# A fused transformer step on one core: the order and the loads of 128 value tiles, with 88 early tiles instead of 64 and whole rows for their second reading

## The reference

```python
def peer_ffn(h, w_query, sub_keys, expert_u, expert_v):
    def block(hb):                                   # 128 tokens
        ...                                          # 8 heads x 16 best of 16,384 experts
        idx = jnp.take_along_axis(cand_i, best_j, axis=-1)
        gate = jax.nn.softmax(best_s, axis=-1)
        u = expert_u[idx]
        act = jax.nn.gelu(jnp.einsum('thkd,td->thk', u, hb))
        coef = (gate * act)
        return jnp.einsum('thk,thkd->td', coef, expert_v[idx])
...
x = x + gt2 * ffn
y = rmsnorm(x, g_final)
```

## Time and profile before

| | us |
|---|---|
| median of 3 runs (lowest, highest) | 3785.51 (3781.29, 3787.98) |
| the profiled execution: its own time | 3779.13 |
| its span | 3777.4 |

### The profile page before, as it was taken

How to read it: one execution, slowest core, us unless ns; L and a number is a source line. 1 busy time by engine, 2 the same in 40 slices (tenths; PEclk the granted TensorE clock), 3 DMA queues, 4 the chain that set the end, 5 groups by cost and what they waited for, 6 DMA issues and landing times.

```text
span 3777.4 us, 28728 instructions
## 1 busy us (share of the span) xinstructions
PE 3104.6 (82%) x9975; PEld 1850.8 (49%) x9975; DVE 2353.0 (62%) x3580; ACT 572.1 (15%) x1365; POOL 980.1 (26%) x779
## 2 busy tenths in 40 slices
PE   4899997979996668796885885359996589999996
PEld 1333443733343434333674553347773257777774
DVE  3110114889986854548777777877777838656653
ACT  0000111121111445402242000420000000000000
POOL 3000001234333421233313323333223314222220
PEclk8999998979998679897996997579998899999998
DMA  9999655889989799988989999889999989999993
GB/s 310 398 361 367 233 200 202 338 319 403 409 330 361 262 401 415 397 296 336 367 292 358 416 416 386 283 341 417 417 417 416 416 333 417 416 417 417 417 411 132
DMA packets 326129, 1344.80 MB, mean 356 GB/s; under 512 B 27625, under 2 KB 76777, under 8 KB 217593
## 3 DMA queue, kind: packets, MB, share of 16 engines
q0 software_dynamic: 106912, 749.72, 49.8%
q1 hardware_dynamic: 166090, 549.84, 37.9%
q10 hardware_dynamic: 52984, 43.42, 3.5%
HBM read 1303.07 MB, written 38.96 MB: 355 GB/s over the span
## 4 chain that ended last, share of the span: by engine, by line
PE 57%; DMA 20%; DVE 15%; issue 4%; ACT 3%; POOL 0%; SPq 0%; ACTq 0%; DVEq 0%; POOLq 0%
PE ps L1023 27%; PE ps L619 7%; DVE arena L2183 7%; DMA arena<-in_expert_u_dram,arena 6%; DMA arena<-in_expert_v_dram 5%; PE ps L778 4%; PE ps L828 4%; DMA arena<-in_cache_k_dram 3%; PE ps L710 3%; PE ps L577 2%; DMA arena<-in_w_ada_dram 2%; DMA arena<-in_w_in_dram 2%; PE ps L607 2%; PE ps L1015 2%; DMA arena<-in_w_out_dram 1%
## 5 line engine op out<-in xcount | busy, mean ns | idle before, releaser
L1023 PE MATMUL ps<-arena 128*128 128x512 f32 x3072 | 1384.4, 611 | 175.2 <-DMA arena<-in_expert_v_dram 116.1
L2183 DVE CUSTOM_DVE_ANT_0 arena<-arena 128x2048 f32<-128x2048 f32 x544 | 1241.7, 2290 | 315.3 <-DMA arena<-in_expert_u_dram,arena 309.5
L1023 PEld LDWEIGHTS ps<-arena 128*128 128x128 f32 x3072 | 943.6, 309 | 615.0 <-issue 270.9
L2448 POOL DMA_INDIRECT arena<-in_expert_u_dram,arena x544 | 760.6, 1398 | 1760.9 <-DVE arena L2183 1567.0
L2096 DVE SCALAR_TENSOR_TENSOR arena<-arena 128x2048 f32<-128x2048 f32 x158 | 371.6, 2352 | 205.3 <-issue 165.8
L828 PE MATMUL ps<-arena 128*128 128x512 f32 x896 | 409.4, 611 | 0.4 <-DVE arena L2027 0.2
L619 PE MATMUL ps<-arena 128*128 128x512 f32 x640 | 288.4, 604 | 9.5 <-DMA arena<-in_w_in_dram 9.5
L828 PEld LDWEIGHTS ps<-arena 128*128 128x128 f32 x896 | 169.7, 195 | 246.6 <-issue 240.1
L2448 POOL DMA_INDIRECT arena<-in_expert_v_dram,arena x160 | 176.7, 1105 | 410.5 <-DVE arena L2096 368.3
L577 PE MATMUL ps<-arena 128*128 128x128 f32 (+3 forms) x954 | 158.4, 319 | 151.7 <-DMA arena<-in_cache_k_dram 50.3
L577 PEld LDWEIGHTS ps<-arena 128*128 128x128 f32 (+3 forms) x954 | 128.0, 169 | 220.2 <-issue 67.7
(11 more groups left out here) (246 smaller groups left out, 1761.1 us busy)
## 6 DMA issues: line engine op xcount, KB each, us to landing
arena<-in_expert_v_dram SPq DMA_DIRECT2D x320, 512.0 KB
arena<-in_w_ada_dram SPq DMA_DIRECT2D x96, 1024.0 KB, 10.5
arena<-in_w_in_dram SPq DMA_DIRECT2D x80, 1024.0 KB, 8.2
arena<-in_w_query_dram SPq DMA_DIRECT2D x36, 1024.0 KB
arena<-dense_coefs SPq DMA_DIRECT2D x48, 768.0 KB
arena<-in_w_out_dram SPq DMA_DIRECT2D x32, 1024.0 KB, 5.1
dense_coefs<-arena ACTq DMA_DIRECT2D x12, 2048.0 KB, 20.4
arena<-in_cache_k_dram SPq DMA_DIRECT2D x24, 1024.0 KB
```

The costliest lines, as they stand in the source:

```text
L1023: ins = MM(ps[:, BANK[half, b] + c, :], weights, dense_v[m % V_DENSE][:, c * NC:(c + 1) * NC], start=(m == FIRST_TILE[half, b]), stop=(m = ...
L2183: V.tensor_tensor_reduce(out=u_slot[s % RING], in0=u_slot[s % RING], in1=h2[b], scale=1.0, scalar=0.0, op0=ALU.mult, op1=ALU.add, accum_ou ...
L2448: nc.gpsimd.indirect_dma_start(out=slot, out_offset=None, in_=table, in_offset=bass.IndirectOffsetOnAxis(ap=idx, axis=0),).then_inc(loaded ...
```

## The change

There are now 88 early tiles. The list is: 88 lower tiles for blocks 0 and 1; the other 40 lower tiles for all three; then for each of the first 88 groups a pair, its lower columns for block 2 and its upper columns for all three, loaded as one transfer of whole rows (1.049 MB) into two neighbouring places of the ring; then 40 upper tiles. Early tiles are due one per 1.2 slots, so that the last eight fall among the quads of block 2. The lower sums of blocks 0 and 1 are copied by ACT from PSUM to `h2` at `T_LOW` = 430, behind a wait for all 128 lower tiles; the lower sums of block 2 stay in PSUM. DVE's `end_low` is gone; `end_block` at `T_HIGH` = 556 does both halves, in operations of 1,024 columns. The residual rows are loaded by SP behind the last tile, no longer by ACT at slot 402. Chunks are loaded for blocks 0 and 1 or for all three, never for block 2 alone.

```diff
-EARLY_TILES = 64
+EARLY_TILES = 88
...
+TILES = [(0, i, (0, 1) if i < EARLY_TILES else (0, 1, 2)) for i in range(NKEY)]
+N_LOW = len(TILES)
+for _i in range(NKEY):
+    if _i < EARLY_TILES:
+        TILES.append((0, _i, (2,)))
+    TILES.append((1, _i, (0, 1, 2)))
+N_PAIRED = N_LOW + 2 * EARLY_TILES
...
-BANK = {(0, 0): 2, (0, 1): 4, (0, 2): 0, (1, 0): 6, (1, 1): 2, (1, 2): 4}
+BANK = {(0, 0): 2, (0, 1): 4, (0, 2): 0, (1, 0): 2, (1, 1): 4, (1, 2): 6}
...
 def t_tile(m):
     if m < EARLY_TILES:
-        return t_quad(1, QUADS) + 3.0 + (C_FROM[2] - t_quad(1, QUADS) - 4.0) * m / EARLY_TILES
-    return t_quad(2, QUADS) + 2.0
...
-T_LOW = 474
-T_HIGH = 569
-T_X1 = 402
+        return t_quad(1, QUADS) + 3.0 + 1.2 * m
+    return max(t_quad(1, QUADS) + 3.0 + 1.2 * EARLY_TILES, t_quad(2, QUADS) + 2.0)
...
+T_LOW = 430
+T_HIGH = 556
...
 # PE, dense()
-                for b in range(DENSE):
-                    if b:
-                        pe.wait_ge(low_free, 2 * b)
-                    for m in range(N_LOW, N_LOW + V_DENSE):
...
+                for m in range(N_LOW, len(TILES)):
                     tile_loaded(m)
-                    for b in range(DENSE):
+                    for b in TILES[m][2]:
+                        if m == N_LOW + 1 and b < 2:
+                            pe.wait_ge(low_free, b + 1)
                         ins = tile_of_block(m, b)
                     ins.then_inc(tile_used, 1)
...
 # ACT, reload()
-                yield T_X1
...
-                for b in range(DENSE):
-                    act.dma_start(h2[b], x1_of[b]).then_inc(x1_back, 16)
+                yield T_LOW
+                act.wait_ge(u_done, 2 * SLOTS)
+                act.wait_ge(tile_used, N_LOW)
+                for b in range(2):
+                    sums = ps[:, BANK[0, b]:BANK[0, b] + 2, :].rearrange("p a n -> p (a n)")
+                    A.copy(h2[b][:, 0:HALF], sums).then_inc(low_free, 1)
...
 # DVE, in place of end_half and end_low
+            def end_block(b):
+                for half in range(2):
+                    cols = slice(half * HALF, (half + 1) * HALF)
+                    sums = ps[:, BANK[half, b]:BANK[half, b] + 2, :].rearrange("p a n -> p (a n)")
+                    if half == 0 and b < 2:
+                        sums = h2[b][:, cols]
+                        dv.wait_ge(low_free, b + 1)
                     link(V.tensor_tensor(sums, sums, gate2_kept[:, cols], ALU.mult))
+                    V.tensor_tensor(h2[b][:, cols], x1_dense[b][:, cols], sums, ALU.add).then_inc(fin_x[0], 1)
...
 # SP
             def load_tile(m):
                 half, i, _ = TILES[m]
+                wide = 2 if is_paired(m) else 1
+                place = m % V_DENSE
                 if m >= V_DENSE:
-                    sp.wait_ge(tile_used, m - V_DENSE + 1)
+                    sp.wait_ge(tile_used, m + wide - V_DENSE)
+                sp.dma_start(at(VD0 + HALF * place, wide * HALF),
+                             v_rows[i * NKEY:(i + 1) * NKEY, half * HALF:(half + wide) * HALF]).then_inc(dv_loaded[place], 16)
...
+            sp.wait_ge(tile_used, len(TILES))
...
+            for b in range(DENSE):
+                sp.dma_start(x1_dense[b], x1_of[b]).then_inc(x1_back, 16)
```

More of the change, by code:

```diff
@@ L132, with is_paired @@
 assert VD0 + V_DENSE * HALF <= Z0
[L135 to L146, removed]
-CHUNK_OF = [sum(1 for a in CHUNK_AT if a <= m) - 1 for m in range(len(TILES))]
-assert EARLY_TILES % JS == 0
+TILES = [(0, i, (0, 1) if i < EARLY_TILES else (0, 1, 2)) for i in range(NKEY)]
[5 more added lines that the diff above has]
+N_PAIRED = N_LOW + 2 * EARLY_TILES
+assert EARLY_TILES % JS == 0 and N_LOW % 2 == 0 and V_DENSE % 2 == 0
+def is_paired(m):
+    return N_LOW <= m < N_PAIRED
+CHUNK_AT = [m for m in range(len(TILES)) if TILES[m][1] % JS == 0 and not (is_paired(m) and TILES[m][0])]
+CHUNK_OF = [sum(1 for a in CHUNK_AT if a <= m) - 1 for m in range(len(TILES))]
+LOADS = [m for m in range(len(TILES)) if not (is_paired(m) and TILES[m][0])]
+TILE_LOADED = {}
+for _n, _m in enumerate(LOADS):
+    _place = _m % V_DENSE
+    _count = sum(1 for a in LOADS[:_n + 1] if a % V_DENSE == _place)
+    for _k in range(2 if is_paired(_m) else 1):
+        TILE_LOADED[_m + _k] = (_place, 16 * _count)
 FIRST_TILE = {(h, b): min(m for m, t in enumerate(TILES) if t[0] == h and b in t[2]) for h in range(2) for b in range(DENSE)}
 LAST_TILE = {(h, b): max(m for m, t in enumerate(TILES) if t[0] == h and b in t[2]) for h in range(2) for b in range(DENSE)}
-BANK = {(0, 0): 2, (0, 1): 4, (0, 2): 0, (1, 0): 6, (1, 1): 2, (1, 2): 4}
+BANK = {(0, 0): 2, (0, 1): 4, (0, 2): 0, (1, 0): 2, (1, 1): 4, (1, 2): 6}
 NEAR = CH - FAR
@@ L375, in trunk_step @@
         dense_v = [at(VD0 + HALF * i, HALF) for i in range(V_DENSE)]
+        x1_dense = [at(CB0 + D * b, D) for b in range(DENSE)]
         u_slot = [at(R0 + D * i, D) for i in range(RING)]
@@ L1497, in finish @@
                             act.wait_ge(fin_sq[1], 1)
-                        square(b, i, v_slot[i][0:NS, 0:HALF] if b == SB else ps[:, 0:2, :].rearrange("p a n -> p (a n)"))
+                        square(b, i, v_slot[i][0:NS, 0:HALF] if b == SB else at(TK0, HALF))
                 if after == LAG + 4:
@@ L2096, in add @@
                     V.scalar_tensor_tensor(out=acc, in0=value, scalar=scale, in1=acc, op0=ALU.mult, op1=ALU.add).then_inc(add_done, 1)
[L2098 to L2101, removed]
-                    link(V.tensor_tensor(sums, sums, gate2_kept[:, cols], ALU.mult))
-                    ins = V.tensor_tensor(h2[b][:, cols], h2[b][:, cols], sums, ALU.add)
-                    if half == 0:
-                        ins.then_inc(low_free, 1)
-                    else:
-                        ins.then_inc(fin_x[0], 1)
-            def end_low():
-                yield T_LOW
-                dv.wait_ge(tile_used, N_LOW)
-                dv.wait_ge(x1_back, 48)
-                dv.wait_ge(kept_loaded, 32)
-                for b in range(DENSE):
-                    end_half(0, b)
+            def end_block(b):
[5 more added lines that the diff above has]
+                        dv.wait_ge(low_free, b + 1)
+                    link(V.tensor_tensor(sums, sums, gate2_kept[:, cols], ALU.mult))
+                    V.tensor_tensor(h2[b][:, cols], x1_dense[b][:, cols], sums, ALU.add).then_inc(fin_x[0], 1)
             def mean(b):
@@ L2167, in end_high @@
                     scale_rows(b)
-            side = Side(choices(), gates(), norm1_b(), mix_b(), attention_b(), sample_scores(), project_out(), build_dense(), end_low(), end_high())
+            side = Side(choices(), gates(), norm1_b(), mix_b(), attention_b(), sample_scores(), project_out(), build_dense(), end_high())
             dv.wait_ge(norm_h, 4)
@@ L2335, in load_chunk @@
             def load_chunk(u):
-                half, i, blocks = TILES[CHUNK_AT[u]]
-                parts = slice(4 * blocks[0], 4 * blocks[-1] + 4)
+                m = CHUNK_AT[u]
+                blocks = 2 if m < EARLY_TILES else DENSE
                 if u >= C_RING:
```

43 lines of the change are left out of this document (18 added, 25 removed).

## The result

| | before | changed |
|---|---|---|
| median of four runs each (lowest to highest) | 3783.4 us (3776.5 to 3788.0) | 3739.5 us (3736.6 to 3744.9) |
| profiled execution, own time / span | 3779.1 / 3777.4 us | 3736.6 / 3734.9 us |

The ratio is 0.9887, with its 95% interval 0.9867 to 0.9907: 1.1% faster. The time lies 2.5 us above the forecast of 3737 us, inside its range and on the side that was given 0.83.

A forecast was written before the change was run, and what follows sets the result against it. DMA sets the pace most of the time; PE finishes last only by its waits, 72 us behind the stream's end. 52 us less behind the last add, 3 us more ahead of it: 3737 us, range 3708 to 3772.

The forecast's parts named there:

- the side that was given 0.83: Whole program: the chance given to the changed kernel being faster, against 0.09 for within 0.2% and 0.08 for slower.
- Behind the last add: Program's end: only the sample's folds, arithmetic, scaling and last store remain, 20 us instead of 72.
- Bytes: Whole program: half tiles +12.6 MB, chunks -5.8 MB, together +6.8 MB or 16 us of full DMA.
- The early tiles: Before PE's second phase: build 5 us later, eight tiles among its quads 2.5 us each, 20 us; second phase at 2536.
- The half clock that I feared: Block 2's build: a tile takes 6.8 us at 1.2 GHz against 3.4 at 2.4; upper bound 8 x 6.8 = 54 us.
- The wait behind the build: Behind block 2's build: residual rows no longer load there, 4 us less, bounds 0 and 7.5.
- a build that pays in full: Rival at block 2's build: half-clock tiles and load waits delay the second phase by 60 us or more; 3776 and above; chance 0.06.
- The hold: Slot 430: stream and gathers held 2709 to 2748, 39 us; gathers in flight cover 28, some 11 load only tiles.
- the 7 us: Slot 430: what the hold adds ahead of the last add in the forecast's sum.
- Pairs: Second phase: 88 pairs at 6.78 us, 597 us; whole rows get at least 184 GB/s; PE's tiles end at 3548.
- The stream to its end: From 2746: DMA-paced at 416.5 GB/s until 3548, gathers until 3631, then DVE 78 us; last add at 3709.
- gathers alone don't fill DMA: Rival after the last tile: at 3.76 us a gather, 54 gathers take 203 us, 3786 us, no change; chance 0.06.

The follow-up runs named there:

- low_436: The changed kernel with `T_LOW` 436 instead of 430, so DVE isn't held at slot 432: 3737.6 us, 0.9878 of the kernel before.
- after_again: The changed kernel run once more, unaltered: 3745.2 us, 0.9918 of the kernel before.
- early_80: The changed kernel with 80 early tiles instead of 88, none among block 2's quads, and the copy at slot 440: 3735.4 us, 0.9863 of the kernel before.
- half_rows: The changed kernel with each pair read as two half tiles of 4 KB rows, same order and bytes: 3792.9 us, 1.0023 of the kernel before.
- no_gate: The changed kernel without the gate multiplication in the dense end, six DVE operations fewer: 3735.1 us, 0.9860 of the kernel before.
- before_88: The kernel before with 88 early tiles and their due times alone, no pairs: 3790.8 us, 1.0025 of the kernel before.
- high_540: The changed kernel with the dense end at slot 540 instead of 556: 3737.7 us, 0.9869 of the kernel before.

## Why the prediction was right, and where its steps were off

**Why the sum came so near.** The path was right: PE done long before the stream, DVE's work as the last bound, 52 us less behind the last add. That the sum is only 2.5 us off is luck in part, since its terms missed by more, in opposite directions. The profiled execution was 8.8 us late before the change could act (its first early tile came at 2061.19, against 2052.43). From there to the second phase it took 13.7 us less than forecast. From the second phase to the last add it took 1185.2 us, where the forecast had 1173 (2536 to 3709), 12.2 more. Behind the last add it took 1.3 us less, and the profiled execution lay 2.9 us under the median, not 6.4.

**Bytes.** As worked out: the page has 1351.61 MB moved against 1344.80.

**The early tiles.** I let the build begin at 2399 and last 110 us; it began at 2410.7 and lasted 96.3 (2410.71 to 2506.96). 8.8 of these 12 us are the late start, so only 3 belong to the change. The build is the mis-sized term: eight tiles among its quads cost 96.3 - 90.4 = 5.9 us, 0.7 each, not 2.5. In the other traces the build took 97 to 99 us with the eight tiles and 91 to 92 without them, so it is 0.5 to 1.1 each. A tile took 3.72 us of PE (six of the eight so), nearly the 3.4 of full clock, and it fell into time in which PE waited for ACT. The half clock that I feared came only in part: three of the eight tiles took 5.4 to 5.6 us in low_436 and in after_again, none did here. The granted clock over the build was 0.89, against 0.65 before. The tiles among the quads are what raised it: early_80 has tiles right ahead of its build too, but none among the quads, and stays at 0.65. The stretch of the build in the changed kernel, then in early_80:

```profile
2411.00:2507.00 96.00, 70.06 (x322) 55.94 (x320) 75.95 (x105) 60.62 (x168) 16.07 (x13) 0.89 0.82 289
```

```profile
2412.00:2504.00 92.00, 55.10 (x259) 49.17 (x259) 78.04 (x105) 60.42 (x167) 17.27 (x15) 0.65 0.75 254
```

The wait behind the build was 24.1 us, against 30.5 before; I had said 4 us less, it was 6.4. In all the second phase began at 2531.1, forecast 2536. The rival of a build that pays in full is refuted.

**The hold.** Forecast on DVE 2709 to 2748, 39 us, of which 11 with only tiles loading; measured 2717.6 to 2741.6, 24 us. DMA didn't fall during the hold (419 and 420 GB/s in the two 10 us stretches ahead of 2740), but just behind it: 356 and 324, some 1.6 MB or 4 us of a full DMA. That the gathers in flight keep DMA full while DVE is held was right, as far as 24 us show it; the hold was shorter than the 28 us that I gave them, so the 11 us of tiles alone never came, and the price fell behind the hold, at half of the 7 us. By low_436 it is 2 to 3.

**Pairs.** Whole rows got 177 GB/s where I needed 184. PE was busy 48.3 to 50 of 50 us, and a pair took 7.04 us instead of 6.78. That is 88 x 0.26 = 23 us, the largest miss of the working: tiles ended at 3564.7, not 3548. Only some 8 us of it are waits for loads (the gaps on PE's timeline with `in_expert_v_dram` as releaser). From 3066.9 to 3316.7 PE had 576 records, 36 pairs, in a row without such a gap, and still took 6.94 us a pair: 0.434 us a record, where the tiles for three blocks have 0.424. Why a record among the pairs is longer no run takes apart. It cost the program little, because PE was no longer last. The choice behind it, to size the share by the cache rows of 8 KB instead of the half rows of 4 KB, is what half_rows tested and bore out. The rule of the Trainium skill ("DMA: Bandwidth & Descriptors", Queues, rings and completion order), that the DMA engines go round their queues packet by packet, agrees with the trace of half_rows: 11203 packets from each queue, and 144.5 GB/s for rows of half the gathers' length. With whole rows it was at least 177, where PE's own pace was nearly the limit. That whole rows could have had 208 no run shows.

**The stream to its end.** I had DVE's last stretch from 3631 to 3709, 78 us; it ran from 3637.4 (the adds back to back) to 3716.2, 78.8 us. The near match is luck in part: 22 adds stood in it, not 24, and some 5 us of waits for gathers took their place. From the end of the hold to its start the sum had 885 us (2746 to 3631); it took 895.8 (2741.6 to 3637.4). Some 4 of these 11 us are the dip behind the hold; the rest stays open. The tiles that still loaded after 3548 don't explain it, for their bytes are in the sum whenever they come. The fear that gathers alone don't fill DMA was unfounded: 421 GB/s from 3550 to 3600 and 410 from 3600 to 3650. That DVE is the bound behind it was argued in the prediction and is shown by no_gate.

**Behind the last add.** 18.7 us for 20, and 71.6 before. Of the 42.5 us that the span lost, 52.9 came from here; 16.5 were given to the later second phase, and the second phase to the last add gave back 6.0.

**What really carried the gain.** With the dense end at slot 556, the new order needs the whole rows: without them (half_rows) PE ends late enough to stop DVE there, and the kernel is 0.2% slower than before. Early tiles in the old order (before_88) bring nothing either, since the single second readings starve. Of the 52.9 us behind the last add, 37.8 are PE's tiles no longer being behind the stream (3705.8 to 3743.6 before), and the rest is what stands ahead of the last add now. How much of the gain the order alone would bring with the dense end at its old place is the open question (see half_rows). The other parts, 24 more early tiles and the exact slots of the copy (430 or 436) and of the dense end (556 or 540), brought nothing that these runs can tell.

## What to carry to other kernels

When one engine waits at the end of a program while DMA was full all along, ask whose loads were starved and by whom: the queue with the short rows loses, and reading the same bytes in rows as long as its rival's may be worth more than reading fewer. Stopping the other stream once, early and late, shows in one run which of the two sets the end. Where the end was bounded by an engine's own work, moving that work about inside the stretch gained nothing here; only taking it out did.

## What the runs showed of the hardware that was not expected

**A gather's issue beside long operations of DVE.** With DVE's adds back to back (2.35 us each), POOL's record for the issue of one gather is 2.5 us long; where DVE had gaps, before, it was 0.95. It is not that DVE is full: at 3666.16 and at 3679.95 the issue took 0.94 us beside operations of the dense end, which follow each other without a gap too, but are 1.22 us long. POOL's timeline of the changed kernel, then that of the kernel before:

```profile
3645.59 2.50 POOL L2450 DMA_INDIRECT arena<-in_expert_v_dram,arena  x1 [2.48 <-DVE arena L2098]
...
3666.16 0.94 POOL L2450 DMA_INDIRECT arena<-in_expert_v_dram,arena  x1 [0.30 <-issue]
```

```profile
3641.76 0.95 POOL L2448 DMA_INDIRECT arena<-in_expert_v_dram,arena  x1 [6.58 <-DVE arena L2096]
```

Between 3560 and 3710 us the mean is 2071 ns over 34 gathers, against 1198 over 28. POOL's spans are rough, and no run here takes the cause apart. The Trainium skill ("SBUF — State Buffer", SBUF: two separate sides) tells of a port pair that DVE and GpSimd share and that some DVE operations hold; the rows would fit it, which is argued, not shown. It may be why the last adds in high_540 waited for their gathers.

**The second phase's start moves from run to run.** Profiled executions with 88 early tiles began it between 2526.4 and 2546.2 us, and their first early tile between 2049.3 and 2076.5 us, with nothing changed ahead of it. A difference of 5 us between two kernels can't be read from their spans alone.
